# Norms over the channels: two of the eight multiplications moved from VectorE to ScalarE and GpSimd

## The chip, the cores and the metric

The kernel runs on one core of one Trainium2 chip. The metric is the device time in microseconds. The kernel before took 4352.61 us (median of 3 runs, 4348.45 to 4368.29). Lower is better.

## The reference

The program computes four layers of a network on one sequence of 512 tokens with 1024 channels: two layers of a first kind (convolution module, differential attention, gated delta net, an MLP), one layer with a spatial gate, RWKV time mixing and a gated MLP, and one with sparse attention, a short convolution and a mixture of experts. The change touches only the norm over the channels that stands between them:

```python
def rms_norm(x, w, eps=NORM_EPS):
    xf = x.astype(jnp.float32)
    y = xf * lax.rsqrt(jnp.mean(xf * xf, axis=-1, keepdims=True) + eps)
    return (y * w.astype(jnp.float32)).astype(x.dtype)
```

Everything is float32. In the first kind of layer the result of the last norm is added to the running sum, `x = x + rms_norm(h, post_mlp_w)`; elsewhere a norm makes the input of the next projection, and the last one makes the output.

## The kernel before

Channels lie on the 128 partitions, so a tensor of 1024 channels by 512 tokens is eight tiles (`KD` = 8) of 128x512 in SBUF. The program is a chain of phases. `phase` (L165 to 172) opens a block in which each engine has its own stream of instructions, ordered by semaphores that are written out by hand. When the block ends, every engine drains, GpSimd gathers the arrivals and clears the semaphores, and all engines meet at a barrier: nothing of the next phase starts before every engine has finished this one.

`rms_norm` (L242 to 312) is one such phase. It runs nine times:

- in each of two passes of the loop over the first kind of layer, once in front of the mixer (L3324) and once behind the MLP with `add_to=mem.x` (L3343);
- at L2222 and L2233 in the third layer, at L2789 and L3009 in the fourth, and at L2800 as the last of all, with `store=out`.

Inside it, VectorE squares the even tiles (L298) and ScalarE the odd ones (L275). TensorE sums over the channels by eight float32 matmuls with a matrix of ones (L288) and then runs 30 matmuls on a constant tile that nothing reads (`fill_in`, L239), or 60 where `add_to` is given. ScalarE takes the logarithm (L278) and the exponential (L281) of the sum, each with a load of its activation table; this gives the factor `scale`, one row of 512 repeated on all partitions. VectorE then multiplies tile by tile, source times the norm's weight (one number per partition) times `scale`, in one instruction each (L306), eight in all; with `add_to` it writes them to `squares`, and adds eight tiles to the running sum (L311). With `store`, the SyncE queue writes each tile out as soon as it is made (L268). With `following`, the first weights of the next phase are loaded and split into two parts (L223 on ScalarE, L230 on VectorE) in this phase. With `vectors`, the norm's weights themselves are loaded at its start (L259). GpSimd has no work in it.

Of the kernel before, what the change touches and what calls it, by code (L numbers as in the profile page):

```python
# [12 lines left out]
ACT = mybir.ActivationFunctionType  # L13
ALU = mybir.AluOpType
# [3 lines left out]
P = 128  # L18
SEQ = 512
D_MODEL = 1024  # L20
KD = D_MODEL // P
# [142 lines left out]
@contextmanager  # L164
def phase(nc, *names):  # L165


    sems = [nc.alloc_semaphore(f"{n}_{nc.next_id()}") for n in names]
    with nc.Block() as block:  # L169
        yield (block, *sems)  # L170
    nc.clear_and_free_semaphores(sems)
    nc.all_engine_barrier()  # L172


@contextmanager
def buffers(nc, **shapes):

    with ExitStack() as stack:
        yield [stack.enter_context(nc.sbuf_tensor(f"{n}_{nc.next_id()}", s, F32)) for n, s in shapes.items()]
# [55 lines left out]
def fill_in(nc, mem, bank, n):  # L235

    tile = mem.filler[:, :]
    for _ in range(n):
        nc.tensor.matmul(bank[:, :], tile, tile.unsqueeze(1).broadcast_to([P, SEQ // P, P]), start=True, stop=True)  # L239


def rms_norm(nc, mem, source, gain, out, add_to=None, following=None, vectors=(), ahead=(),  # L242
             store=None):

    with buffers(nc, squares=[P, KD, SEQ], scale=[P, SEQ]) as (squares, scale), phase(
            nc, "vectors_loaded", "ahead_loaded", "act_squares", "dve_squares", "sum_ready", "logged", "root_ready",
            "made", "stored", "dve_steps", *Primer.SEMS) as (  # L250
            block, vectors_loaded, ahead_loaded, act_squares, dve_squares, sum_ready, logged, root_ready, made, stored,
            dve_steps, *primer_sems):
        total = mem.bank[0]
        primer = Primer(nc, mem, following, primer_sems)

        @block.sync
        def _(sp):
            for to, data in vectors:
                sp.dma_start(to, data).then_inc(vectors_loaded, 16)  # L259
            for to, data in ahead:  # L260
                sp.dma_start(to, data).then_inc(ahead_loaded, 16)
            primer.load(sp)
            if ahead:
                sp.wait_ge(ahead_loaded, 16 * len(ahead))
            if store is not None:
                for k in range(KD):
                    sp.wait_ge(made, k + 1)
                    sp.dma_start(store[:, k, :], out[:, k, :]).then_inc(stored, 16)  # L268
                sp.wait_ge(stored, 16 * KD)

        @block.scalar
        def _(act):

            for k in range(1, KD, 2):
                nc.scalar.activation(squares[:, k, :], source[:, k, :], ACT.Square).then_inc(act_squares, 1)  # L275
            primer.high(act)
            act.wait_ge(sum_ready, 1)
            nc.scalar.activation(scale[:, :], total[:, :], ACT.Ln, bias=mem.eps[:, 0:1],  # L278
                                 scale=1.0 / D_MODEL).then_inc(logged, 1)
            act.wait_ge(logged, 1)  # L280
            nc.scalar.activation(scale[:, :], scale[:, :], ACT.Exp, scale=-0.5).then_inc(root_ready, 1)  # L281

        @block.tensor
        def _(pe):

            for k in range(KD):
                pe.wait_ge(act_squares if k % 2 else dve_squares, k // 2 + 1)
                last = nc.tensor.matmul(total[:, :], CONST(mem.const, "ones"), squares[:, k, :],  # L288
                                        start=(k == 0), stop=(k == KD - 1))
            last.then_inc(sum_ready, 1)  # L290
            fill_in(nc, mem, mem.bank[1], 30 if add_to is None else 60)

        @block.vector
        def _(dve):
            steps = Steps(dve, dve_steps)

            for k in range(0, KD, 2):
                steps.did(nc.vector.tensor_tensor(squares[:, k, :], source[:, k, :], source[:, k, :], ALU.mult),  # L298
                          dve_squares)
            primer.low(dve)  # L300
            dve.wait_ge(root_ready, 1)
            if vectors:
                dve.wait_ge(vectors_loaded, 16 * len(vectors))
            for k in range(KD):
                to = out if add_to is None else squares
                steps.did(nc.vector.scalar_tensor_tensor(out=to[:, k, :], in0=source[:, k, :], scalar=gain(k),  # L306
                                                         in1=scale[:, :], op0=ALU.mult, op1=ALU.mult), made)
            if add_to is not None:
                steps.settle()
                for k in range(KD):  # L310
                    steps.did(nc.vector.tensor_tensor(add_to[:, k, :], add_to[:, k, :], squares[:, k, :], ALU.add))  # L311
            steps.settle()


# [1897 lines left out]
def second_even(nc, mem, a):  # L2212
    with buffers(nc, vec=[P, VECE.size]) as (vec,):
        with buffers(nc, y=[P, KD, SEQ], u=[P, UTE, SEQ], gates=[P, 3, RW_PAIRS, SEQ]) as (y, u, gates):
            decay, rate, gate = [gates[:, i, :, :] for i in range(3)]

            w_tm = gates[:, :, :, :].rearrange("p i j s -> p (i j s)")[:, 0:KD * A_WIDTH]

            pv = y[:, A_GROUPS:KD, :].rearrange("p t n -> p (t n)").rearrange("p (t n) -> p t n", n=A_WIDTH)
            with split_ring(nc, mem):  # L2220
                w_in = Weights(unit_of(a["w_ine"]), UTE // 2, 2, KD)
                rms_norm(nc, mem, mem.x, lambda k: VECE(vec, "norm_mix", k), mem.h,  # L2222
                         vectors=[(vec[:, :], a["vece"])], ahead=[(w_tm, a["w_tme"])])
                token_major(nc, mem, w_tm, A_WIDTH, mem.h, pv, w_in)
                project(nc, mem, w_in, mem.h, copy_out(nc, u), primed=SPLIT)
            spatial_gate(nc, mem, a, vec, u, pv, y, decay, rate, gate)
            w_out = Weights(unit_of(a["w_oute"]), KD // 2, 2, KD)
            time_mix(nc, mem, vec, u, y, decay, rate, gate, w_out)
            with split_ring(nc, mem):
                project(nc, mem, w_out, y, add_out(nc, mem.x), on_vector=True, primed=LOADED)  # L2230
        ff = FeedForward(unit_of(a["w_ffe"]), unit_of(a["w_downe"]), FFN_T, "silu")
        with split_ring(nc, mem):
            rms_norm(nc, mem, mem.x, lambda k: VECE(vec, "norm_ffn", k), mem.h, following=ff.up[0])  # L2233
            feed_forward(nc, mem, ff, lambda half: add_out(nc, mem.x), lambda half: True)
# [547 lines left out]
def second_odd(nc, mem, a, out):  # L2782
    with buffers(nc, vec=[P, VECO.size]) as (vec,):
        with buffers(nc, y=[P, KD, SEQ], u=[P, UTO, SEQ], tm=[P, TT, TMO], rope=[P, 2, SEQ], k_cmp=[P, C_KV, N_CMP],
                     v_cmp=[P, C_KV, HEAD]) as (y, u, tm, rope, k_cmp, v_cmp):
            with split_ring(nc, mem):
                w_in = Weights(unit_of(a["w_ino"]), UTO // 2, 2, KD)
                with buffers(nc, w_tm=[P, KD * TMO]) as (w_tm,):
                    rms_norm(nc, mem, mem.x, lambda k: VECO(vec, "norm_mix", k), mem.h,  # L2789
                             vectors=[(vec[:, :], a["veco"])],  # L2790
                             ahead=[(w_tm[:, :], a["w_tmo"]), (rope[:, :, :], a["rope"])])
                    token_major(nc, mem, w_tm, TMO, mem.h, tm, w_in)
                project(nc, mem, w_in, mem.h, copy_out(nc, u), primed=SPLIT)
            w_out = Weights(unit_of(a["w_outo"]), KD // 2, 2, KD)
            compress(nc, mem, a, vec, rope, u, y, k_cmp, v_cmp, w_out)
            sparse_attention(nc, mem, rope, u, tm, k_cmp, v_cmp, y)
            with split_ring(nc, mem):
                project(nc, mem, w_out, y, add_out(nc, mem.x), on_vector=True, primed=LOADED)
        mixture(nc, mem, a, lambda k: VECO(vec, "norm_ffn", k))
        rms_norm(nc, mem, mem.x, lambda k: VECO(vec, "final", k), mem.h, store=out)  # L2800
# [695 lines left out]
```

## Time and profile before

| | us |
|---|---|
| median of 3 runs | 4352.61 |
| profiled execution, its own time | 4353.19 |
| span of the profiled execution | 4351.4 |
| PE busy | 4042.6 |
| DVE busy | 1538.4 |
| ACT busy | 1324.1 |
| POOL busy | 224.6 |

PE is TensorE's matmuls, PEld its weight loads, DVE VectorE, ACT ScalarE, POOL GpSimd, SPq the queue in which SyncE issues transfers. Each engine's busy time is the sum of its instructions' durations. The ends of matmuls are modelled, and spans on POOL are rough. An instruction's duration includes a tail that overlaps with the one behind it, so a row of several instructions is shorter than their durations added up. The share of span between the profiled execution's time and its span (1.8 us) lies outside the first and last instruction.

### The profile page before, as it was taken

The numbers are of one execution on the slowest core, as the hardware profiler recorded it, in microseconds if no ns is written. First come the engines' busy times: TensorE is split into PE (matmuls) and PEld (weight loads), VectorE is DVE, ScalarE is ACT, GpSimd is POOL, SyncE is SP. The second block draws the span as 40 slices with busy tenths as digits, with TensorE's granted clock in tenths as the row PEclk, the third lists the DMA queues.
The fourth block names the chain that finished last, engine by engine and source line by source line (L and its number), as shares of the span: only waits on it lengthen the run. The fifth ranks groups of instructions, "written<-read, shape, count | busy, mean of one in ns | idle before, by whom it ended". The sixth has DMA issues, their size and how long they took to land. (4 is left out here: it accounts for less than half of the span.)

```text
span 4351.4 us, 56361 instructions
## 1 busy us (share of the span) xinstructions
PE 4042.6 (93%) x21923; PEld 3378.8 (78%) x21923; DVE 1538.4 (35%) x2718; ACT 1324.1 (30%) x2282; POOL 224.6 (5%) x187
## 2 busy tenths in 40 slices
PE   8999999999999999999997889999998879999999
PEld 5787786787677878678766777787775669999998
DVE  2365444332326454433234554332224421111121
ACT  2364443232236444323123332322222311111111
POOL 0150100000015010000000000000000000000000
PEclk9998889999999888999999899999997879999999
DMA  3100011221210001122221002232230014554544
GB/s 123 43 1 1 0 39 66 89 97 58 82 47 1 1 0 39 58 97 87 68 78 44 1 16 72 79 101 82 86 116 1 20 67 176 203 215 177 214 176 147
DMA packets 54647, 333.48 MB, mean 77 GB/s; under 512 B 7600, under 2 KB 8496, under 8 KB 23520
## 3 DMA queue, kind: packets, MB, share of 16 engines
q1 hardware_dynamic: 51904, 324.95, 21.2%
q0 software_dynamic: 2592, 6.49, 0.6%
q8 instruction: 98, 1.61, 0.2%
q14 instruction: 53, 0.43, 0.0%
HBM read 326.17 MB, written 4.19 MB: 76 GB/s over the span
## 5 line engine op out<-in xcount | busy, mean ns | idle before, releaser
L501 PE MATMUL bank<-high 128*128 128x512 f32 x2480 | 976.0, 394 | 44.9 <-DVEq L591 22.8
L502 PE MATMUL bank<-low,high 128*128 128x512 f32 x2480 | 972.1, 392 | 0.0
L503 PE MATMUL bank<-high,low 128*128 128x512 f32 x2480 | 971.7, 392 | 0.0
L501 PEld LDWEIGHTS bank<-high 128*128 128x128 f32 x2480 | 470.7, 190 | 151.0 <-DVEq L591 25.7
L502 PEld LDWEIGHTS bank<-low,high 128*128 128x128 f32 x2480 | 470.9, 190 | 97.8
L503 PEld LDWEIGHTS bank<-high,low 128*128 128x128 f32 x2480 | 470.0, 190 | 98.8
L561 DVE TENSOR_TENSOR low<-weight_ring,high 128x2048 fp32r<-128x2048 f32 (+1 forms) x144 | 319.3, 2218 | 545.7 <-ACT high L518 545.7
L3124 PE MATMUL bank<-chosen,glu_ring 128*128 128x176 f32 x2816 | 424.5, 313 | 0.0
L3124 PEld LDWEIGHTS bank<-chosen,glu_ring 128*128 128x128 f32 x2816 | 421.4, 190 | 0.0
L518 ACT ACTIVATE high<-weight_ring 128x2048 fp32r<-128x2048 f32 (+1 forms) x144 | 266.8, 1854 | 266.2 <-PE bank L503 232.4
L239 PE MATMUL bank<-filler 128*128 128x512 f32 x819 | 243.3, 440 | 20.6 <-PEq L172 19.9
L239 PEld LDWEIGHTS bank<-filler 128*128 128x128 f32 x819 | 165.0, 205 | 73.8 <-issue 38.3
L3138 PE MATMUL bank<-hidden,down_ring 128*128 128x176 f32 x1408 | 211.3, 313 | 0.0
L3138 PEld LDWEIGHTS bank<-hidden,down_ring 128*128 128x128 f32 x1408 | 210.4, 190 | 0.0
L1414 DVE TENSOR_TENSOR joint<-bank,level_masks 128x512 f32<-128x512 f32 x224 | 153.9, 691 | 148.5 <-PE bank L1433 148.5
L741 POOL TENSOR_TENSOR y<-y,scaled 128x512 f32<-128x512 f32 x120 | 149.7, 1276 | 997.6 <-ACT scaled L775 997.6
L3246 DVE TENSOR_TENSOR hidden<-silu,bank 128x176 f32<-128x176 f32 x88 | 29.8, 338 | 385.7 <-ACT silu L3202 385.7
L3202 ACT ACTIVATE silu<-bank 128x176 f32<-128x176 f32 x88 | 27.9, 318 | 448.5 <-PE bank L3124 448.5
L569 DVE TENSOR_TENSOR gated<-gated,bank 128x512 f32<-128x512 f32 x86 | 59.0, 686 | 282.5 <-ACT gated L525 157.9
L1446 PE MATMUL bank<-weight_ring,joint 128*128 128x128 f32 x1152 | 153.1, 277 | 0.0
L622 ACT ACTIVATE u<-bank 128x512 f32 (+1 forms) x84 | 50.3, 599 | 330.4 <-PE bank L503 330.4
L1446 PEld LDWEIGHTS bank<-weight_ring,joint 128*128 128x128 f32 x1152 | 140.7, 193 | 0.9
(503 smaller groups left out, 4738.6 us busy)
## 6 DMA issues: line engine op xcount, KB each, us to landing
glu_ring<-in_w_expert SPq DMA_DIRECT2D x88, 1024.0 KB, 4.9
weight_ring<-in_w_ff SPq DMA_DIRECT2D x64, 1024.0 KB, 5.0
down_ring<-in_w_expert_down SPq DMA_DIRECT2D x64, 704.0 KB, 5.1
weight_ring<-in_w_in SPq DMA_DIRECT2D x22, 1024.0 KB, 4.8
weight_ring<-in_w_ffe SPq DMA_DIRECT2D x22, 1024.0 KB, 4.8
weight_ring<-in_w_downe SPq DMA_DIRECT2D x16, 704.0 KB, 4.0
weight_ring<-in_w_ino SPq DMA_DIRECT2D x11, 1024.0 KB, 4.9
weight_ring<-in_w_ine SPq DMA_DIRECT2D x9, 1024.0 KB, 4.9
```

Of the source, the lines that this page charges most:

```text
L239: nc.tensor.matmul(bank[:, :], tile, tile.unsqueeze(1).broadcast_to([P, SEQ // P, P]), start=True, stop=True)
L501: nc.tensor.matmul(mem.bank[b][:, :], whole, high[:, k, :], start=(k == 0), stop=False)
L502: nc.tensor.matmul(mem.bank[b][:, :], whole, low[:, k, :], start=False, stop=False)
L503: last = nc.tensor.matmul(mem.bank[b][:, :], rest, high[:, k, :], start=False, stop=(k == kt - 1))
L518: nc.scalar.activation(w_high[:, s, :], mem.ring[:, s, 0:size], ACT.Copy).then_inc(high_ready[s], 1)
L561: nc.vector.tensor_tensor(w_low[:, s, :], mem.ring[:, s, 0:size], w_high[:, s, :], ALU.subtract).then_inc(low_ready[s], 1)
L569: nc.vector.tensor_tensor(whole, whole, mem.bank[b][:, :], ALU.mult).then_inc(taken[b], 1)
L741: nc.gpsimd.tensor_tensor(y[:, c, :], y[:, c, :], scaled[:, n % CONV_SLOTS, :], ALU.add).then_inc(added, 1)
L1414: nc.vector.tensor_tensor(chunks(joint[:, n, :]), chunks(turn_bank(i)[:, :]), mask, ALU.mult) \
L1446: last = nc.tensor.matmul(product_bank(i)[:, c], joint[:, n, c], matrix[:, n, c], start=True, stop=True)
L3124: last = nc.tensor.matmul(two(low[s])[:, half, :], glu_ring[:, s, at:at + P], chosen[:, k, :], start=(k == 0), stop=(k == KD - 1))
L3138: last = nc.tensor.matmul(two(high[m // 2])[:, m % 2, :], down_ring[:, s, k * P:(k + 1) * P], hidden[:, k, :], start=(k == 0), stop=(k == ...
```

## The change

In every call of `rms_norm` the last two of the eight tiles go another way. ScalarE multiplies them by the norm's weights (into a new buffer `gained`) behind its squares and in front of its wait for the sum; where the weights are loaded in this phase, it waits for them first. GpSimd multiplies them by `scale` when the factor is there, and, with `add_to`, also adds these two tiles to the running sum. VectorE does six tiles instead of eight, in both loops. The stores of the last two tiles wait for GpSimd. `add_norm`, the norm that the first kind of layer has in front of its MLP, is unchanged.

```diff
+POOL_FROM = KD - 2
...
-    with buffers(nc, squares=[P, KD, SEQ], scale=[P, SEQ]) as (squares, scale), phase(
+    with buffers(nc, squares=[P, KD, SEQ], gained=[P, KD - POOL_FROM, SEQ], scale=[P, SEQ]) as (
+            squares, gained, scale), phase(
...
                 for k in range(KD):
-                    sp.wait_ge(made, k + 1)
+                    if k < POOL_FROM:
+                        sp.wait_ge(made, k + 1)
+                    else:
+                        sp.wait_ge(pool_made, k - POOL_FROM + 1)
                     sp.dma_start(store[:, k, :], out[:, k, :]).then_inc(stored, 16)
...
             primer.high(act)
+            if vectors:
+                act.wait_ge(vectors_loaded, 16 * len(vectors))
+            for k in range(POOL_FROM, KD):
+                nc.scalar.activation(gained[:, k - POOL_FROM, :], source[:, k, :], ACT.Copy, scale=gain(k)) \
+                    .then_inc(act_gained, 1)
             act.wait_ge(sum_ready, 1)
...
-            for k in range(KD):
+            for k in range(POOL_FROM):
                 to = out if add_to is None else squares
...
-                for k in range(KD):
+                for k in range(POOL_FROM):
                     steps.did(nc.vector.tensor_tensor(add_to[:, k, :], add_to[:, k, :], squares[:, k, :], ALU.add))
+            steps.settle()
+
+        @block.gpsimd
+        def _(pool):
+            steps = Steps(pool, pool_steps)
+            pool.wait_ge(root_ready, 1)
+            pool.wait_ge(act_gained, KD - POOL_FROM)
+            for k in range(POOL_FROM, KD):
+                to = out if add_to is None else squares
+                steps.did(nc.gpsimd.tensor_tensor(to[:, k, :], gained[:, k - POOL_FROM, :], scale[:, :], ALU.mult),
+                          pool_made)
+            if add_to is not None:
+                steps.settle()
+                for k in range(POOL_FROM, KD):
+                    steps.did(nc.gpsimd.tensor_tensor(add_to[:, k, :], add_to[:, k, :], squares[:, k, :], ALU.add))
             steps.settle()
```

## Rows read from the trace of the kernel before

**Rows 1.** The page: busy time of each engine; TensorE's granted clock in 40 slices.

```profile
PE 4042.6 (93%) x21923; PEld 3378.8 (78%) x21923; DVE 1538.4 (35%) x2718; ACT 1324.1 (30%) x2282; POOL 224.6 (5%) x187
PEclk9998889999999888999999899999997879999999
```

**Rows 2.** One source line, L306: durations min/median/max in ns, first and last start.

```profile
L306 DVE SCALAR_TENSOR_TENSOR h_branch<-x_res,vec,scale x56: 743/747/753, 27.7 to 4347.5; 128x512 f32<-128x512 f32 x56
```

**Rows 3.** Timeline of the first norm: start, us, engine, line, [idle before, releaser].

```profile
15.00 2.19 ACT L275 ACTIVATE squares<-x_res 128x512 f32<-128x512 f32 x4 [0.74 <-PEq L172]
...
24.46 7.38 PE L239 MATMUL bank<-filler 128*128 128x512 f32 x30
...
25.06 0.69 ACT L278 ACTIVATE scale<-bank,const_cols 128x512 f32<-128x512 f32 x1 [6.57 <-PE bank L288]
...
27.07 0.63 ACT L281 ACTIVATE scale<-scale 128x512 f32<-128x512 f32 x1
27.73 5.39 DVE L306 SCALAR_TENSOR_TENSOR h_branch<-x_res,vec,scale 128x512 f32<-128x512 f32 x8 [10.19 <-ACT scale L281]
...
34.20 8.12 PE L647 MATMUL bank<-w_tm,h_branch 128*128 128x408 f32 x23 [2.36 <-PEq L172]
```

**Rows 4.** Timeline of a norm with add_to, and the start of the next.

```profile
1092.45 14.21 PE L239 MATMUL bank<-filler 128*128 128x512 f32 x60
...
1095.72 5.39 DVE L306 SCALAR_TENSOR_TENSOR squares<-h_branch,vec,scale 128x512 f32<-128x512 f32 x8 [9.79 <-ACT scale L281]
1101.22 4.91 DVE L311 TENSOR_TENSOR x_res<-x_res,squares 128x512 f32<-128x512 f32 x8
...
1111.72 5.68 PE L288 MATMUL bank<-squares,const_cols 128*128 128x512 f32 x8 [5.06 <-DVE squares L298]
```

**Rows 5.** Timeline of the norm that also prepares the next phase's weights.

```profile
2683.89 1.92 ACT L223 ACTIVATE high<-weight_ring 128x2048 fp32r<-128x2048 f32 x1 [3.45 <-DMA weight_ring<-in_w_ffe]
2685.83 1.28 ACT L278 ACT_TABLE_LOAD   x1
...
2687.88 0.69 ACT L278 ACTIVATE scale<-bank,const_cols 128x512 f32<-128x512 f32 x1 [0.77 <-PE bank L288]
...
2697.02 1.38 PE L239 MATMUL bank<-filler 128*128 128x512 f32 x5 [2.33 <-PEq L172]
```

**Rows 6.** Timelines: transfers issued back to back, and the stores of the last norm.

```profile
3535.68 0.33 SPq L2862 DMA_DIRECT2D router<-in_router  x1
3536.06 0.43 SPq L2863 DMA_DIRECT2D bias<-in_router_b  x1
...
4343.68 4.97 SPq L268 DMA_DIRECT2D out<-h_branch  x8
```

**Rows 7.** Timeline of a stretch in which GpSimd and VectorE work at once.

```profile
349.68 3.96 DVE L1287 SCALAR_TENSOR_TENSOR weight_ring<-bank,pair_cols,weight_ring 128x128 f32<-128x128 f32 x15
350.62 5.01 POOL L1300 TENSOR_TENSOR weight_ring<-weight_ring,const_cols 128x512 f32<-128x512 f32 x4 [53.81 <-DVE weight_ring L1287]
353.55 2.48 DVE L1292 TENSOR_TENSOR weight_ring<-bank,weight_ring 128x512 f32<-128x512 f32 x4
```

**Rows 8.** The tile `vec` in the norm at 3079 us: its load, and time to landing.

```profile
L259 SPq DMA_DIRECT2D vec<-in_veco x1: 339/339/339, 3079.2 to 3079.2; - x1
...
DMA to landing us min/median/max: 3.6/3.6/3.6
```

**Rows 9.** TensorE behind a gap; stretches: us, busy by engine, granted clock, DMA share, GB/s.

```profile
2631.35 0.77 PE L501 MATMUL bank<-high 128*128 128x512 f32 x1 [3.58 <-DVE low L597]
...
34.00:38.00 4.00, 3.81 (x11) 2.20 (x12) 0.00 (x0) 0.00 (x0) 0.00 (x0) 1.00 0.69 231
...
2631.30:2634.70 3.40, 3.35 (x8) 2.70 (x9) 3.40 (x6) 2.94 (x4) 0.00 (x0) 0.51 0.90 308
...
809.50:815.40 5.90, 5.89 (x14) 4.64 (x15) 2.29 (x1) 1.77 (x1) 0.00 (x0) 0.50 0.68 201
...
993.20:996.30 3.10, 3.10 (x8) 2.44 (x9) 1.47 (x1) 1.59 (x1) 0.00 (x0) 0.51 0.63 174
```

More of the change, by code:

```diff
@@ L239, in fill_in @@
         nc.tensor.matmul(bank[:, :], tile, tile.unsqueeze(1).broadcast_to([P, SEQ // P, P]), start=True, stop=True)
+POOL_FROM = KD - 2
 def rms_norm(nc, mem, source, gain, out, add_to=None, following=None, vectors=(), ahead=(),
              store=None):
-    with buffers(nc, squares=[P, KD, SEQ], scale=[P, SEQ]) as (squares, scale), phase(
+    with buffers(nc, squares=[P, KD, SEQ], gained=[P, KD - POOL_FROM, SEQ], scale=[P, SEQ]) as (
+            squares, gained, scale), phase(
             nc, "vectors_loaded", "ahead_loaded", "act_squares", "dve_squares", "sum_ready", "logged", "root_ready",
-            "made", "stored", "dve_steps", *Primer.SEMS) as (
+            "made", "stored", "act_gained", "pool_made", "pool_steps", "dve_steps", *Primer.SEMS) as (
             block, vectors_loaded, ahead_loaded, act_squares, dve_squares, sum_ready, logged, root_ready, made, stored,
-            dve_steps, *primer_sems):
+            act_gained, pool_made, pool_steps, dve_steps, *primer_sems):
         total = mem.bank[0]
```

## The prediction, made before the changed kernel ran

> **What bounds the kernel now.** I read the page first. TensorE is busy 93% of the span, at a granted clock of 0.9 of full speed or so, and VectorE 35% [rows 1]. That says little about the norms, where TensorE's busy time is mostly filler. So I went by the source line of the multiplications, which shows where the nine norms are and that an instruction there lasts 747 ns always [rows 2], and then by the timeline of each norm. All nine have one shape. In the first [rows 3] the sum is ready at 25.06, logarithm, table load and exponential end at 27.70, and the eight multiplications run from 27.73 to 33.12. TensorE's filler ends at 31.84. The next phase's first matmul stands at 34.20, 1.08 us behind VectorE's end. So VectorE is what arrives last at the barrier, with TensorE 1.28 us ahead of it. The reader should see both distances: the first is the price of a barrier, which stays; the second is the most that VectorE can give back.
>
> The eight multiplications take 5.39 us, so they start (5.39 - 0.747)/7 = 0.663 us apart, and two of them are worth 1.33 us, not 1.49.
>
> With add_to it is otherwise [rows 4]. VectorE ends its adds at 1101.22 + 4.91 = 1106.13, and the 60 filler matmuls end at 1092.45 + 14.21 = 1106.66. There TensorE is last, and time taken from VectorE is worth nothing.
>
> In the last norm the end is set by the stores: eight are issued in 4.97 us, at VectorE's pace [rows 6], and the phase waits until the last has landed.
>
> **The change part by part.**
>
> *ScalarE's copies.* Four squares take 2.19 us, 0.52 us apart [rows 3], so two copies of the same shape cost 1.04 us. They stand in front of the table load and of the wait for the sum. In the first norm ScalarE then idles 6.57 us until the sum is there, and about 6 us in most of the others: hidden. The wait for the weights hides too. Queued behind it are the copies, the table load and the logarithm, for which TensorE's sum waits for nobody, and the weights land 3.6 us after their issue at 3079.2 [rows 8], at 3082.8, with copies (1.04, and 0.11 of tail) and table load (1.28) at an end by 3085.2, while that norm's logarithm starts at 3087.18. The one exception is the norm that splits weights [rows 5]: the split ends at 2685.81, the copies move the table load to 2686.87, it ends at 2688.15, and the logarithm stands at 2687.88 now. That costs 0.28 us, once.
>
> *VectorE.* It loses two multiplications per norm (1.33 us), and two adds in each of the two norms with add_to, 2 x 0.60 us from (4.91 - 0.69)/7.
>
> *GpSimd.* It gets two multiplications per norm, and two adds in two norms. Four of its instructions of this shape take 5.01 us [rows 7], 1.25 us each, so it needs 2.5 us from the moment the factor is there; alone it would be done at 30.3 in the first norm, before anybody else. Clearing three more semaphores costs nothing that I can price, since the clearing is one instruction over a range.
>
> *Both at once, the cost the trace doesn't show.* The question is whether VectorE keeps its pace beside GpSimd. In rows 7 it does: fifteen instructions of L1287 in 3.96 us, 0.26 us apart with and without GpSimd beside them, and GpSimd's four are evenly spaced. But VectorE reads a PSUM bank there for one of its two tensors, and so it does in every stretch of the trace in which the two engines overlap. In the norm both tensors of L306 (`x_res` or `h_branch`, and `scale`), and both of L311, lie in SBUF, and so do GpSimd's. No row has that pair. What speaks for a clash is that GpSimd needs 1.25 us for two SBUF tensors that VectorE's add takes in 0.60 us, as if its operands came in by turns.
>
> So I bound it. From below: no clash, the norm is as long as TensorE's filler, a gain of 1.28 us. From above: whoever has the way in holds it for its whole instruction. Then VectorE's six (5 x 0.663 + 0.747 = 4.06 us) and GpSimd's two (2.50 us) stand one behind the other in whatever order, 6.57 us in place of 5.39: a loss of 1.18 us. With add_to, 4.06 + 0.11 (the pause between the two loops) + 3.70 (six adds) + 5.01 (four on GpSimd) = 12.88 us in place of 10.41, a loss of 2.47 us, of which TensorE's 0.53 us lead of rows 4 hides a part: 1.94 us. The rows nearest in kind (rows 7) are for the lower end; but they lack the very thing in question, and I take the upper end.
>
> The Trainium skill has a rule for this pair ("SBUF — State Buffer", § Who interferes with whom): a VectorE instruction with two SBUF inputs contends with a GpSimd instruction that reads SBUF, because its second input comes through the read interface that the two share, and the second to issue blocks fully. By it the upper end holds; it is also consistent with rows 7, where one input is in PSUM. No row of the kernel before tests the part of it that matters here.
>
> *TensorE's clock behind a longer gap.* If the norm ends 1.18 us later, TensorE waits between filler and next phase not 2.36 us but 3.5. Five norms have such a gap of 2.3 us with dense work behind it, the first [rows 3] to that at 2697.02 [rows 5] and one more at 3096; behind them the clock stays at 1.00, as 34 to 38 us shows [rows 9]. Behind a gap of 3.58 us at 2631.35 it is 0.51, that is the lower level of 1.2 GHz, for 3.4 us, and behind longer gaps likewise for 5.9 us (from 809.5) and 3.1 us (from 993.2) [rows 9]. Half of such a stretch is lost where TensorE is busy throughout: 1.7, 2.95 and 1.55 us, 2.1 us in the mean. At gaps of 3.5 us I count three of the five: 6.2 us, with 0 and 5 x 2.95 = 14.8 us as the ends.
>
> **The sum.** Six norms at 1.18 = 7.1; two with add_to at 1.94 = 3.9; the last norm 1.2, since the last store waits for the last tile; the late table load 0.3. That is +12.4 us, and with the clock +18.7. On the profiled execution's 4353.2 us (span 4351.4 and 1.8 around it) this gives 4371.9; the median lies 0.6 lower, so 4371.
>
> **The rivals.**
>
> *Side by side.* No clash. Six norms gain 1.28 us each, held by the filler's end: 7.7. The two with add_to gain nothing, since TensorE is last there. The last norm gains the pace of two stores: 0.38 us apart as two issues in a row are, in place of 0.663 [rows 6], 0.57 us. Less 0.3 for the table load: -8.0 us, 4345. For it speak rows 7 and every other overlap; against it, that none of them has the operands of the norm.
>
> *Longer than serial, the clock at every norm.* Same place, but the clock falls at all five gaps, and low stretches are as long as the longest row: 12.4 + 14.8 = +27 us, 4380. It decides from the third or fourth fall on: with 12.4 us of serial work, a 4374 needs 9.5 us of clock. For it: the row behind 3.58 us. Against: this gap is a little shorter, and is one case.
>
> *A part of the clash.* GpSimd holds the way in for only some of its 1.25 us (it also has to decode and compute). Half of it would be about 1.25 us less per norm, back at the time before: 4353. Nothing in the rows supports a share, so this has little weight. That the change doesn't do what it says can't be in another way: the split of tiles is fixed, and all of GpSimd's operands are ready early.
>
> **How the numbers follow.** Serial with up to four clock falls: 0.47, from 4364 to 4376. Side by side: 0.33, 4342 to 4348. Clock at every norm: 0.13. A part of the clash: 0.07. A measurement of this kernel tells about 0.5% (22 us) from no change. Faster by more than that (below 4331) needs more than all VectorE time in question: 0.02. Slower by more (above 4374): the third case and the upper end of the first, 0.13 + 0.10 = 0.23. The rest, 0.75, is within. The likeliest case's own range is 4364 to 4376; since cases of both signs are in play, the range is 4342 to 4382.
>
> **What would show it.** In the timeline of the first norm of the changed kernel: six multiplications on VectorE and two on GpSimd from about 27.7. If they clash, VectorE's six take more than 4.1 us or GpSimd's two stand behind them or last well over 1.25 us, and the next phase starts 6.4 to 6.7 us behind the factor plus 1.1 for the barrier (near 35.4, now 34.20). If they don't, VectorE ends near 31.8, TensorE's filler at 31.84, and the next phase starts at 32.9. The norms with add_to should start their successor 1.9 us later, or not move at all. The gap in front of the next matmul (2.36 now) should read 3.5 or 1.1, with a granted clock of 0.5 or 1.00 in the 4 us behind it. The split norm's logarithm should start 0.28 us later against its sum. I am wrong if VectorE keeps 0.663 us between starts beside GpSimd; then everything but the 0.3 falls, and the sign with it.

## The result, and the profile after

The changed kernel takes 4358.48 us (median of 20 runs, 4346.45 to 4373.81) against 4346.15 us (20 runs, 4337.12 to 4368.29) for the kernel before: ratio 1.0024, 95% interval 1.0014 to 1.0034. By the ratio that is a loss of 10.4 us (6 to 15); the two medians lie 12.3 us apart. The forecast had the sign and a loss of 18.7 us, so its size was nearly double. Its 4371 us was too high by another 6.5 us, since it stood on 4352.61 us, the median of three runs of the kernel before; with 20 runs that median is 4346.15. The profiled execution took 4354.26 us, with a span of 4352.5.

The first two lines of the page, which answer to [rows 1], show nothing of this; GpSimd has 33 us more work and VectorE, with 22 instructions fewer, 9 us more:

```profile
PE 4037.5 (93%) x21923; PEld 3366.2 (77%) x21923; DVE 1547.4 (36%) x2696; ACT 1334.5 (31%) x2300; POOL 258.0 (6%) x209
...
PEclk9998999999999899999998899999996779999999
```

An engine that has lost 14 us of work and got busier is being held up. The timeline of the first norm shows where, beside [rows 3] (columns: start, us, engine, line, operation, what ended the idle time before):

```profile
24.70 7.41 PE L239 MATMUL bank<-filler 128*128 128x512 f32 x30
25.30 0.69 ACT L290 ACTIVATE scale<-bank,const_cols 128x512 f32<-128x512 f32 x1 [5.73 <-PE bank L300]
...
27.97 6.27 DVE L318 SCALAR_TENSOR_TENSOR h_branch<-x_res,vec,scale 128x512 f32<-128x512 f32 x6 [10.57 <-ACT scale L293]
28.01 3.02 POOL L333 TENSOR_TENSOR h_branch<-gained,scale 128x512 f32<-128x512 f32 x2 [27.57 <-ACTq L169]
35.34 1.02 PE L674 MATMUL bank<-w_tm,h_branch 128*128 128x408 f32 x1 [3.24 <-PEq L172]
```

Six multiplications take 6.27 us where eight took 5.39. In the rows of the two lines (durations in ns, min/median/max) the reader sees that most of VectorE's are as short as ever and a few last 1.9 us, and that GpSimd's, 1.25 us alone [rows 7], go up to 1.76:

```profile
L318 DVE SCALAR_TENSOR_TENSOR h_branch<-x_res,vec,scale x42: 736/740/1904, 28.0 to 4347.3; 128x512 f32<-128x512 f32 x42
```

```profile
L333 POOL TENSOR_TENSOR h_branch<-gained,scale x14: 1286/1524/1755, 28.0 to 4343.1; 128x512 f32<-128x512 f32 x14
```

Instruction by instruction, in all seven norms without add_to, VectorE starts at 2.67, 4.48, 6.18, 6.84, 7.50 and 8.16 us behind the logarithm's start (within 0.05) and ends at 8.92; before it was 2.67 to 8.06 in equal steps. GpSimd starts at 2.71 and 3.97. The first two instructions of VectorE are held; once GpSimd has done, the pace is 0.66 us again.

The norms with add_to, beside [rows 4]:

```profile
1079.49 14.21 PE L239 MATMUL bank<-filler 128*128 128x512 f32 x60
...
1082.75 8.30 DVE L318 SCALAR_TENSOR_TENSOR squares<-h_branch,vec,scale 128x512 f32<-128x512 f32 x6 [9.78 <-ACT scale L293]
1082.80 2.98 POOL L333 TENSOR_TENSOR squares<-gained,scale 128x512 f32<-128x512 f32 x2 [545.52 <-ACTq L169]
1085.86 3.33 POOL L338 TENSOR_TENSOR x_res<-x_res,squares 128x512 f32<-128x512 f32 x2
1091.17 3.70 DVE L323 TENSOR_TENSOR x_res<-x_res,squares 128x512 f32<-128x512 f32 x6
```

Here four products and sums on GpSimd hold four multiplications of VectorE; GpSimd is done before VectorE's adds begin. VectorE ends at 1094.87, TensorE's filler at 1093.70: 1.17 us later than the filler, which was last before. At the second such norm this has a further effect. The norm behind it, at 2192 us, begins with the sum over the channels, for which its logarithm waits, and TensorE's gap in front of that sum goes from 1.81 us to 3.15. The sum in the first trace of before, in its second trace, and in the changed kernel:

```profile
2200.78 8.83 PE L288 MATMUL bank<-squares,const_cols 128*128 128x512 f32 x16 [1.81 <-DVE squares L298]
```

```profile
2187.95 7.13 PE L288 MATMUL bank<-squares,const_cols 128*128 128x512 f32 x16 [1.69 <-DVE squares L298]
```

```profile
2182.28 10.03 PE L300 MATMUL bank<-squares,const_cols 128*128 128x512 f32 x16 [3.15 <-DVE squares L310]
```

The granted clock in the first 4 us of this sum is 0.57, 1.00 and 0.50.

The last norm issues its eight stores in 5.68 us, not 4.97 [rows 6], because the two tiles of GpSimd, ready early, are queued behind VectorE's last. The last store lands 12.42 us behind the logarithm, where it was 10.29:

```profile
4341.82 6.23 DVE L318 SCALAR_TENSOR_TENSOR h_branch<-x_res,vec,scale 128x512 f32<-128x512 f32 x6 [11.16 <-ACT scale L293]
4341.87 2.98 POOL L333 TENSOR_TENSOR h_branch<-gained,scale 128x512 f32<-128x512 f32 x2 [82.57 <-ACTq L169]
4343.73 5.68 SPq L275 DMA_DIRECT2D out<-h_branch  x8
```

And the clock behind the norms. Four stretches of 4 us behind a gap, of the changed kernel, beside the row from 34 us in [rows 9] (columns: stretch, us, busy by engine, granted clock, DMA share, GB/s):

```profile
35.30:39.30 4.00, 3.96 (x6) 2.19 (x7) 0.00 (x0) 0.00 (x0) 0.00 (x0) 0.50 0.74 240
1120.80:1124.80 4.00, 3.97 (x6) 2.18 (x7) 0.00 (x0) 0.00 (x0) 0.00 (x0) 0.50 0.72 236
2202.30:2206.30 4.00, 3.95 (x6) 1.83 (x7) 0.00 (x0) 0.00 (x0) 0.00 (x0) 0.64 0.77 252
3080.50:3084.50 4.00, 3.93 (x17) 3.23 (x18) 0.00 (x0) 0.00 (x0) 0.00 (x0) 1.00 0.75 252
```

At 0.50 (the 1.2 GHz level) TensorE does six matmuls where it did eleven.

For the sums below I took the length of each of the 71 phases from one clearing of semaphores by GpSimd to the next, in the trace of each kernel, and added up three groups: the nine norms; the six phases behind those without add_to and store; and the 56 others, which nothing touches. Against the first trace of before, the changed kernel has +15.2, +9.9 and -23.9 us. Its second trace has +13.8, +5.6 and -9.7, and a second trace of before +0.7, +3.4 and -8.2. On the mean of two traces each, the changed kernel is 14.2 us longer in the norms, 6.0 in the phases behind them, and 12.8 shorter in the others.

### The profile page after: what moved, and what is told of

Its sections match the earlier page's. It is cut to its first block and busy times, and to the rows that moved or that the text cites. A ratio compares the mean times of both kernels' runs of the same rounds, so it can differ in the third digit from the quotient of the medians.

```text
span 4352.5 us, 56397 instructions
## 1 busy us (share of the span) xinstructions
PE 4037.5 (93%) x21923; PEld 3366.2 (77%) x21923; DVE 1547.4 (36%) x2696; ACT 1334.5 (31%) x2300; POOL 258.0 (6%) x209
```

## The experiments

**The factor in PSUM.** VectorE's multiplications get one input from a bank; GpSimd waits for the copy in SBUF, `factor`, and reads that:

```diff
-            nc.scalar.activation(scale[:, :], scale[:, :], ACT.Exp, scale=-0.5).then_inc(root_ready, 1)
+            nc.scalar.activation(root[:, :], scale[:, :], ACT.Exp, scale=-0.5).then_inc(root_ready, 1)
+            nc.scalar.activation(factor[:, :], scale[:, :], ACT.Exp, scale=-0.5).then_inc(factor_ready, 1)
...
-                steps.did(nc.vector.scalar_tensor_tensor(out=to[:, k, :], in0=source[:, k, :], scalar=gain(k),
-                                                         in1=scale[:, :], op0=ALU.mult, op1=ALU.mult), made)
+                steps.did(nc.vector.scalar_tensor_tensor(out=to[:, k, :], in0=root[:, :], scalar=gain(k),
+                                                         in1=source[:, k, :], op0=ALU.mult, op1=ALU.mult), made)
```

> The changed kernel, but the exponential writes the factor twice: first into a PSUM bank, from which VectorE takes it, then into a buffer of SBUF for GpSimd (which starts 0.5 us later). VectorE's six multiplications then have one input in SBUF and one in PSUM; GpSimd's work is the same. Clash of two SBUF inputs: VectorE's six are 0.66 us apart beside GpSimd as without it, they end near 6.8 us behind the start of the logarithm (8.94 in the changed kernel, 8.06 before), the next matmul stands near 7.9, and the time falls to about 8 us below the kernel before (ratio 0.998). Rival, GpSimd disturbs VectorE whatever the operands: VectorE's first two last 1.8 us again, and the time is that of the changed kernel (1.0024).

Measured: 4330.04 us (10 runs), ratio 0.9955 (0.9939 to 0.9972). Its first norm:

```profile
24.11 7.38 PE L239 MATMUL bank<-filler 128*128 128x512 f32 x30
24.72 0.69 ACT L290 ACTIVATE scale<-bank,const_cols 128x512 f32<-128x512 f32 x1 [4.97 <-PE bank L301]
...
27.36 4.04 DVE L319 SCALAR_TENSOR_TENSOR h_branch<-bank,vec,x_res 128x512 f32<-128x512 f32 x6 [9.79 <-ACT bank L293]
27.95 2.60 POOL L334 TENSOR_TENSOR h_branch<-gained,factor 128x512 f32<-128x512 f32 x2 [27.51 <-ACTq L169]
32.51 1.95 PE L675 MATMUL bank<-w_tm,h_branch 128*128 128x408 f32 x5 [1.02 <-PEq L172]
```

The same instructions side by side on both engines, and VectorE takes 4.04 us, its unhindered pace; GpSimd's two are undisturbed as well. What clashed was VectorE's second input in SBUF; GpSimd's work is the same as in the changed kernel. The timed gain, 20 us (12 to 27), is more than the 8 that the norms account for (-7.6 us in its trace); in that trace the rest stands in the third group, -20.5 us, which nothing in the edit touches.

**GpSimd beside all eight, reading, and writing only.** The kernel before with two GpSimd instructions per norm added, into a buffer that nobody reads:

```diff
+                steps.did(nc.gpsimd.tensor_tensor(spare[:, k - KD + 2, :], source[:, k, :], scale[:, :], ALU.mult))
```

> The kernel before with all eight multiplications on VectorE, and beside them two products of two SBUF tensors on GpSimd (source times factor) into a buffer that nobody reads. Clash of inputs: VectorE's first instructions last 1.8 to 1.9 us as in the changed kernel, and its eight end 2.2 us later than before (near 10.3 us behind the logarithm, 8.06 before). Rival, the slowness in the changed kernel comes from the operands' place or from the copies: the eight stay 0.66 us apart.

```diff
+                steps.did(nc.gpsimd.memset(spare[:, k - KD + 2, :], 0.0))
```

> As the last one, but GpSimd only fills the two tiles of the spare buffer with zeros: it writes to SBUF and reads nothing there. If what clashes is the reading of a second input, VectorE's eight stay 0.66 us apart and end at 8.06. If GpSimd's writes or its mere activity hold VectorE up, the first ones last longer, by up to GpSimd's own 1 to 1.3 us.

Measured, one run each: with the reading one 4371.68 us, with the writing one 4361.76 (before, timed beside them, 4346.17, the median of 17; single runs spread over 30 us, so the traces decide). Beside the products, VectorE's instructions go up to 1.9 us and its eight end 10.23 us behind the logarithm, 2.17 us late, as expected:

```profile
L306 DVE SCALAR_TENSOR_TENSOR h_branch<-x_res,vec,scale x56: 734/739/1902, 28.3 to 4366.0; 128x512 f32<-128x512 f32 x56
```

Beside the writes it is as in [rows 3], to the hundredth:

```profile
27.73 5.39 DVE L306 SCALAR_TENSOR_TENSOR h_branch<-x_res,vec,scale 128x512 f32<-128x512 f32 x8 [10.11 <-ACT scale L281]
27.76 0.99 POOL L319 MEMSET spare<- 128x512 f32 x2 [27.32 <-ACTq L169]
```

So it is GpSimd's reading of SBUF against VectorE's reading of a second input there. These two writes, 0.5 us each beside VectorE's first two instructions, hold nothing up.

**One behind the other.** GpSimd waits for VectorE's six (`pool.wait_ge(made, POOL_FROM)`), which is the serial sum of the prediction.

> The changed kernel, with GpSimd waiting until VectorE has done its six multiplications. Nothing overlaps, so this is the serial sum that the prediction took: VectorE ends at 6.73 us behind the logarithm, GpSimd's two products (1.25 us each, as alone) at about 9.3. If the clash is a full lock, this is 0.35 us longer than the changed kernel's 8.94 only because GpSimd's products have lead-in and tail outside the lock there. If VectorE in the changed kernel lost more than GpSimd's working time, this norm would end before 8.94.

```profile
28.30 4.06 DVE L318 SCALAR_TENSOR_TENSOR h_branch<-x_res,vec,scale 128x512 f32<-128x512 f32 x6 [10.94 <-ACT scale L293]
32.50 2.48 POOL L334 TENSOR_TENSOR h_branch<-gained,scale 128x512 f32<-128x512 f32 x2 [32.06 <-PEq L169]
35.99 1.70 PE L675 MATMUL bank<-w_tm,h_branch 128*128 128x408 f32 x2 [3.55 <-PEq L172]
```

The norm ends 9.35 us behind the logarithm, 0.43 us behind the changed kernel's 8.92. VectorE's six take 4.06 us alone and 6.27 beside two products: each product takes 1.10 us away, not its whole 1.25. In the two norms with add_to something does overlap: VectorE goes on to its adds while GpSimd multiplies and adds, four of them are held (starts at 7.45, 9.15, 10.85 and 12.56 us behind the logarithm, the end at 14.33), and so an add with two inputs in SBUF is held like a multiplication. (One run took 4345.43 us; its third group is 33 us shorter than in the first trace of before, its first two 25.7 us longer.)

**The copies alone.** ScalarE's part stays, VectorE multiplies `gained` by the factor itself, behind its six (and does all the adds), and GpSimd's block is gone:

```diff
+            dve.wait_ge(act_gained, KD - POOL_FROM)
+            for k in range(POOL_FROM, KD):
+                steps.did(nc.vector.tensor_tensor(to[:, k, :], gained[:, k - POOL_FROM, :], scale[:, :], ALU.mult), made)
```

> Only ScalarE's part: it still multiplies the last two tiles by the norm's weights, but VectorE multiplies them by the factor (a plain product of two tensors), and GpSimd has nothing. If the copies are hidden but for the norm that splits weights, the norms are as long as before or 0.1 us shorter (two instructions of 0.60 in place of 0.66 us), that one 0.2 us longer, ratio 1.000. If the copies delay the logarithm elsewhere, the time from the squares to the logarithm grows by up to 1 us in each of the nine norms (ratio up to 1.002).

Measured: 4352.74 us (12 runs), ratio 1.0007 (0.9989 to 1.0025). No difference shown. In the norm that splits weights the logarithm starts 0.01 us behind its table load, so it is late there, and that phase is 0.3 us longer (19.08, was 18.77). The copies are not the cause of the loss.

**The clock alone.** The kernel before with four filler matmuls fewer, which nobody waits for:

```diff
-            fill_in(nc, mem, mem.bank[1], 30 if add_to is None else 60)
+            fill_in(nc, mem, mem.bank[1], 26 if add_to is None else 60)
```

> The kernel before, nothing on GpSimd, with 26 filler matmuls in place of 30 in the norms without add_to. Nothing waits for them: the gap in front of the next matmul goes from 2.33 to 3.26 us, and all else is as before. If that gap is what lets the clock fall, the four or five phases behind these norms are 1.4 to 2.9 us longer, 6 to 10 us in all (ratio 1.0015 to 1.002). If the clock in the trace after came from something else, the ratio is 1.000.

Measured: 4364.54 us (8 runs), ratio 1.0037 (1.0019 to 1.0055). Its norms are as long as before (-0.3 us in sum), its gaps 3.24 us, and the phases behind them 6.7 us longer. That is within the 6 to 10 us expected; the timed loss, 16 us (8 to 24), is above them, and the trace doesn't show where the rest lies (third group +2.4):

```profile
34.20:38.20 4.00, 3.92 (x7) 2.15 (x8) 0.00 (x0) 0.00 (x0) 0.00 (x0) 0.62 0.69 233
1123.20:1127.20 4.00, 4.00 (x8) 2.18 (x9) 0.00 (x0) 0.00 (x0) 0.00 (x0) 0.64 0.71 248
2690.10:2694.10 4.00, 3.97 (x9) 3.13 (x10) 3.12 (x6) 3.78 (x8) 0.00 (x0) 0.50 0.55 168
```

**The clash without the gap.** The changed kernel with the filler at 34 and 65:

> The changed kernel with 34 filler matmuls in place of 30, and 65 in place of 60 with add_to: TensorE's gap in front of the next phase goes back from 3.23 us to 2.3, and VectorE's end (8.94 us behind the logarithm) is still the last at the barrier. If the clock behind the longer gap costs what the trace after suggests (about 1.4 to 2.9 us at four norms), the granted clock stays at 1.00 in the 6 us behind those norms, and of the 10 us lost some 6 to 8 come back (ratio near 1.0007). If the clock is not part of it, or falls there anyway, the ratio stays near 1.0024.

Measured: 4343.83 us (12 runs), ratio 0.9993 (0.9976 to 1.0011). The norms keep their clash (+10.8 us), the gaps are 2.3 us again (one 2.68), the clock is low behind one of five, and the second group is back from +9.9 to +1.0. The gap in front of the sum at 2184 us is 2.00 us, and that sum takes 7.13 us:

```profile
34.70:38.70 4.00, 3.99 (x12) 2.32 (x13) 0.00 (x0) 0.00 (x0) 0.00 (x0) 1.00 0.69 236
1125.50:1129.50 4.00, 3.98 (x12) 2.32 (x13) 0.00 (x0) 0.00 (x0) 0.00 (x0) 1.00 0.71 240
```

With four (and five) more matmuls that compute nothing, no loss is shown any more: 13 us came back where 6 to 8 were expected. With the run before it this shows that a good part of what the change costs is the clock and not VectorE's time. It doesn't show that the clock is all of it: the first two groups of this trace are still at +11.8 us, and it is the third, at -19.1, that makes up for them.

**The gap closed in the kernel before.** Filler at 35:

> The kernel before with 35 filler matmuls in place of 30, whose end then stands at VectorE's end; the gap in front of the next matmul goes from 2.33 to about 1.2 us, and nothing is later. If gaps of 2.3 us let the clock fall in some executions (two of them did in the run with the copies alone), this is 3 to 8 us faster than the kernel before (ratio 0.998 to 0.9993), and explains why the factor in PSUM, whose gap is 1.0 us, gained 20 us and not 8. If not, the ratio is 1.000.

Measured: 4340.6 us (12 runs), ratio 0.9984 (0.9968 to 1.0). The interval touches 1, so a gain of 7 us is likely and not shown.

**Both kernels again**, unchanged, for a second trace each:

> The kernel before, unchanged, once more under the profiler. The phases that the change doesn't touch were 24 us shorter in the trace after than in that of before, and 19 to 30 us in the three other kernels with two products on GpSimd, but within 15 us of it in the five kernels without. If that is chance (where the clock falls in the delta and attention phases), this run's untouched phases can lie anywhere between; if it belongs to the kernels, they are within 15 us of the first trace of before.

> The changed kernel, unchanged, once more under the profiler. Chance: untouched phases anywhere from 30 us below to some us above those of the first trace of before. A matter of the kernel: 19 to 30 us below again. The norms themselves end 8.94 us behind the logarithm again, and the clock has fallen behind at least two of the five norms with dense work behind them.

Measured: 4349.22 and 4362.8 us. The norms repeat (8.93 us). Behind the five gaps the clock is low three times in the changed kernel and twice in the kernel before. The third group is -8.2 in the kernel before and -9.7 in the changed one: they don't lie apart here.

**Longer norms without clash or gap.** The kernel before with filler at 39 and 66:

> The kernel before with 39 filler matmuls in place of 30, and 66 in place of 60 with add_to. TensorE now ends the norms itself, 0.9 us behind VectorE without add_to and 1.4 us later than before with it: the norms are about as much longer as in the changed kernel (0.9 and 1.3 us), with no clash, nothing on GpSimd and no long gap. Its own terms add up to +9 us, less the 5 us or so that closing the gap gains. If the 10 us by which the phases that nobody touched are shorter in kernels with the change come from the shift of everything behind the norms, they are 10 to 20 us shorter here as well, and the ratio is 0.998 or less. If they belong to GpSimd's work or to chance, the untouched phases are within 10 us of the first trace of before, and the ratio is near 1.001.

```profile
24.76 9.45 PE L239 MATMUL bank<-filler 128*128 128x512 f32 x39
...
28.03 5.39 DVE L306 SCALAR_TENSOR_TENSOR h_branch<-x_res,vec,scale 128x512 f32<-128x512 f32 x8 [10.74 <-ACT scale L281]
34.98 1.27 PE L647 MATMUL bank<-w_tm,h_branch 128*128 128x408 f32 x3 [0.77 <-PEq L172]
```

Measured: 4344.99 us (12 runs), ratio 0.9992 (0.9972 to 1.0012). Its own groups are +6.7 and -0.2 us, the third -17.1. The trace fell on the side of the shift; the ratio lies between both expectations and settles nothing.

**A version that beats both.** The factor in PSUM, and in the norms with add_to VectorE's products in PSUM as well, since the factor alone left a clash there (its adds read two SBUF tensors and took up to 1.8 us beside GpSimd's); the stores go out in the order in which the tiles are ready:

```diff
+        products = [mem.bank[b] for b in (0, 3, 4, 5, 6, 7)]
...
-                for k in range(KD):
+                for k in (0, 1, 6, 2, 3, 7, 4, 5):
...
-            fill_in(nc, mem, mem.bank[1], 30 if add_to is None else 60)
+            fill_in(nc, mem, mem.bank[1], 30 if add_to is None else 47)
...
-                to = out if add_to is None else squares
+                to = out[:, k, :] if add_to is None else products[k][:, :]
```

> The kernel with the factor in PSUM, and the norms with add_to freed of the clash that it still has there: VectorE writes its six products to PSUM banks and adds them from there, so its adds have one SBUF input too; 47 filler matmuls in place of 60 in these norms; and in the last norm the stores go out in the order in which the tiles are ready. The adds end near 10.5 us behind the logarithm (11.8 with the factor alone, 13.1 before), the two norms are 3 us shorter each, the last store is issued 0.7 us earlier: 6 to 7 us below the kernel with the factor in PSUM (ratio to before near 0.994). If the clock or the next phase takes it back, the ratio stays at 0.9955.

Measured: 4318.18 us (6 runs), ratio 0.9940 (0.9920 to 0.9961), 26 us below the kernel before. A norm with add_to:

```profile
1071.99 11.25 PE L239 MATMUL bank<-filler 128*128 128x512 f32 x47
1072.59 0.69 ACT L291 ACTIVATE scale<-bank,const_cols 128x512 f32<-128x512 f32 x1 [4.92 <-PE bank L302]
...
1075.23 4.05 DVE L320 SCALAR_TENSOR_TENSOR bank<-bank,vec,h_branch 128x512 f32<-128x512 f32 x6 [9.76 <-ACT bank L294]
1075.82 2.54 POOL L335 TENSOR_TENSOR squares<-gained,factor 128x512 f32<-128x512 f32 x2 [546.81 <-ACTq L169]
1078.44 2.58 POOL L340 TENSOR_TENSOR x_res<-x_res,squares 128x512 f32<-128x512 f32 x2
1079.39 3.67 DVE L325 TENSOR_TENSOR x_res<-x_res,bank 128x512 f32<-128x512 f32 x6
```

No instruction is held; VectorE ends 10.47 us behind the logarithm, 13.08 before. The new order of the stores brought nothing: the last is issued 0.34 us earlier than in the kernel with the factor in PSUM, and lands 10.26 us behind the logarithm in both.

## Why the prediction was right and wrong

*The clash: right.* Its choice between [rows 7] and the upper bound is decided by four experiments: second input in PSUM, none; GpSimd writing, none; GpSimd reading beside VectorE with two SBUF inputs, full effect with and without the rest of the change. The rule of the Trainium skill that the prediction quoted ("SBUF — State Buffer", § Who interferes with whom) holds in this kernel as to which operands clash. As to how long, it does not quite: a product holds VectorE up for 1.10 us of its 1.25, not for the whole time that the trace gives to the instruction. And that the second to issue is the one that waits isn't borne out: by the records VectorE's first starts 0.04 us ahead of GpSimd's and is held all the same (spans on GpSimd are rough), while in the last norm of the run with 34 fillers, with starts 0.06 us apart in the same order, it was let through and the next two were held.

*The price of the clash: too high.* One step that failed in size is "whoever has the way in holds it for its whole instruction". In VectorE's ends, six norms were to lose 1.18 us each and lost 0.84 to 0.88, 5.2 us in place of 7.1. The two with add_to were to lose 1.94 and lost 1.17 and 1.20, 2.4 in place of 3.9: four instructions at 1.06 instead of 1.25. The last norm lost 2.1 in place of 1.2: I had overlooked that the stores of GpSimd's tiles queue behind VectorE's last. Late table load: nothing where 0.3 was put, since in this trace the weights landed 0.8 us sooner (the copies-alone run shows the 0.3). In sum 9.7 us in place of 12.4. By the lengths of the phases, from the logarithm to the clearing, it is 10.7: the clearing stands 0.3 us behind TensorE where that is last and 0.6 us behind VectorE, and the norm that splits weights is 0.35 us longer still, for which I have no cause.

*The clock behind the five gaps: right, and about as large as put.* Three falls at 2.1 us were put. The gaps came out at 3.24 us, one at 3.59. The five dense phases behind them have a shortest length each (23.65, 23.65, 29.28, 124.6 and 16.72 us) and are 1.4 to 2.9 us longer when the clock has fallen. Over the two traces of the changed kernel, the one with 26 fillers and the serial one, that is so behind 15 of 20 gaps of 3.2 to 3.6 us. What the prediction had wrong is the other side: it took gaps of 2.3 us as safe from one trace, and behind 7 of 25 of them (before twice, 34 fillers, copies alone, GpSimd's writes; 2.2 to 2.7 us) the clock fell too. At 1.0 to 1.4 us (35 fillers, both versions with PSUM) none of 15 did, and at 0.8 us (39 fillers) none of 5. So the change moved the odds from about one in four to three in four. The two traces of the changed kernel average 7.7 us in this group, those of before 1.7: 6.0 us, and 6.2 were put. (1.3 of the 6.0 stands behind the sixth norm, whose gap was 5.3 us already and is now 6.2.)

*A gap left out.* The prediction counted five gaps, and overlooked the one between the second norm with add_to and the norm right behind it, though it made that gap 1.94 us longer. Over all 14 traces the sum behind it takes 7.13 us nine times and 8.83 once where the gap is 1.7 to 2.0 us, and 9.9 to 10.0 us in all four where it is 3.15 to 3.6 (the changed kernel twice, GpSimd beside eight, one behind the other). That is 2.9 us, and 2.0 on the mean of two traces each, since one of the two traces of before had a low clock there too. The other 1.5 us by which the norms differ stand in front of the logarithms of the first, the third and the last; they vary between traces of the same kernel as well.

*The step that failed: all else held fixed.* In the places that the change touches, the traces have 14.2 us in the norms and 6.0 behind them, 20 us, against 18.7 put. That this comes so near is luck: the clash was priced some 2 us too high, and a gap worth some 2 us was left out. Measured were 10 us (6 to 15). The sum put every other phase at nothing, without a reason, and that term failed: those 56 phases are 12.8 us shorter on the mean of two traces each. They differ within one kernel too. In six traces without products on GpSimd in the norms and with the filler at 26 to 35 the third group is at +3.2 to -8.2 us against the first trace of before, in seven with them at -9.7 to -33.4, and in the one with 39 fillers and no GpSimd at -17.1. Where these phases differ, it is the clock again. The time that they spend at the low clock, worked out from the granted clock of each, is 507 and 490 us in the two traces of before and 453 and 484 in those of the changed kernel; the extremes are 433 us (one behind the other, -33.4) and 525 (writing only, +3.2). The phase at 601 us begins, in the kernel before,

```profile
602.01 3.78 PE L996 MATMUL bank<-y,const_cols 128*128 128x512 f32 x4 [2.62 <-PEq L172]
```

and in the changed one, with the same instructions behind the same gap,

```profile
596.03 1.98 PE L1023 MATMUL bank<-y,const_cols 128*128 128x512 f32 x4 [2.62 <-PEq L172]
```

and is 31.77 and 27.63 us long. The timed runs lean against pure chance: the changed kernel's 20 runs have about half of what its own places cost in the traces, and the versions with PSUM gain at least 12 and 17 us by their intervals, where their norms and the phases behind them make up about 10 and 15, each from one trace. What makes the low clock rarer there, a change of length in front of these phases or something else, is open. Their medians, 20 and 26 us below the kernel before, rest on it in part.

*The rivals.* Side by side (0.33) was refuted in the place where it had its price, and is what the factor in PSUM then did: VectorE's end at 6.68 us, TensorE's filler at 6.78, the next phase at 7.79, with 7.6 us gained against the 8.0 that this rival gave. The clock at every norm (0.13) did not happen: four and three of the five gaps in the two traces. A part of the clash (0.07) had a grain of truth, 12% and not half.

## What to carry to other kernels

Before moving elementwise work from VectorE to GpSimd, look where the operands lie: if VectorE reads two SBUF tensors while GpSimd reads any, they take turns, and each GpSimd instruction costs VectorE nearly its own length; one operand in PSUM makes them independent. When the phase behind a stall belongs to TensorE, price the gap and not only the stall: with the gap filled up to 1.4 us or less, the low clock behind it came in none of 20 cases here. And look for every such gap, also one inside the chain of norms. An overlap seen in a trace is evidence only for the operands it was seen with. And a small change in a long kernel is not the sum of its own places: what nobody touched moved by as much as the effect itself.

## What the runs showed of the hardware that was not expected

- Both sides of the clash are stretched: with a second product queued, GpSimd's goes from 1.28 to 1.75 us, while VectorE's first two last 1.9 and 1.8 us.
- Four filler matmuls more or less, about 0.9 us of TensorE time that nobody waits for, moved the kernel by +16 us (1.0037, from before) and by about -13 us (0.9993 against 1.0024), as much as the 14 us of VectorE's work in question. The traces account for about 7 and 10 us of it.
- An exponential written to PSUM and read from there by VectorE costs nothing: 0.60 us against 0.63 on ScalarE, 0.66 us from start to start on VectorE as from SBUF.
